# A two-layer encoder trunk in float32r: the first half of each down projection over 512 and 128 tokens instead of twice 320

## What is computed

```python
def _swiglu(x, w_gate, w_up, w_down):        # 1024 -> 2816 -> 1024
    return (jax.nn.silu(x @ w_gate) * (x @ w_up)) @ w_down
...
h = h + 0.5 * _rmsnorm(_swiglu(_rmsnorm(h, g[0]), f1g, f1u, f1d), g[1])
```

## Time and profile before

| what | value |
|---|---|
| median of 2 runs | 2795.7 us (2792.97 to 2798.44) |
| span of the profiled execution | 2795.9 us |
| PE busy | 2757.9 us, 99% |
| DVE busy | 1245.5 us, 45% |
| ACT busy | 849.1 us, 30% |
| POOL busy | 447.1 us, 16% |

### The profile page before, as it was taken

One profiled execution on the slowest core, in us unless ns is written; L12 is line 12 of the kernel. 1 busy time (PEld: TensorE's weight loads), 2 busy tenths in 40 slices (PEclk: granted clock), 3 DMA queues, 4 the chain that ended last, 5 costly groups with the idle time before them and its releaser, 6 DMA issues.

```text
span 2795.9 us, 54256 instructions
## 1 busy us (share of the span) xinstructions
PE 2757.9 (99%) x18682; PEld 2719.4 (97%) x18682; DVE 1245.5 (45%) x1997; ACT 849.1 (30%) x1331; POOL 447.1 (16%) x473
## 2 busy tenths in 40 slices
PE   8999999999999999999999999999999999999998
PEld 8999999989999999999999999999899999999997
DVE  5332333674444733233453333355644455333335
ACT  4221223333333522122332122233333343212223
POOL 3100112240001410011321001132300032100112
PEclk9999999999999999999999999999999999999998
DMA  3232222122223222222222222221122222222222
GB/s 104 75 90 86 73 82 71 48 61 66 74 73 91 59 73 81 66 75 87 65 70 75 83 83 75 86 73 50 46 75 75 77 76 61 75 83 76 74 79 89
DMA packets 425146, 208.44 MB, mean 75 GB/s; under 512 B 42425, under 2 KB 423323, under 8 KB 424987
## 3 DMA queue, kind: packets, MB, share of 16 engines
q1 hardware_dynamic: 421956, 203.46, 25.3%
q10 hardware_dynamic: 3062, 3.38, 0.4%
HBM read 203.28 MB, written 5.29 MB: 75 GB/s over the span
## 4 chain that ended last, share of the span: by engine, by line
PE 94%; DVE 3%; issue 1%; ACT 0%; POOL 0%; DVEq 0%; DMA 0%; SPq 0%; ACTq 0%; POOLq 0%
PE ps L540 30%; PE ps L541 29%; PE ps L542 29%; DVE h L1198 1%; DVE x_lo L1180 1%; PE ps L593 1%; PE ps L641 1%; PE ps L588 1%; PE ps L589 1%; PE ps L663 1%; PE ps L521 1%; DVE w_lo L1162 0%; PE ps L527 0%; POOL acc_y L1580 0%; PE ps L691 0%
## 5 line engine op out<-in xcount | busy, mean ns | idle before, releaser
L540 PE MATMUL ps<-x_hi,w_hi 128*128 128x320 f32 x3648 | 1136.6, 312 | 0.0
L542 PE MATMUL ps<-x_hi,w_lo 128*128 128x320 f32 x3648 | 1127.2, 309 | 0.0
L541 PE MATMUL ps<-x_lo,w_hi 128*128 128x320 f32 x3648 | 1127.0, 309 | 0.0
L540 PEld LDWEIGHTS ps<-x_hi,w_hi 128*128 128x128 f32 x3648 | 684.8, 188 | 11.4 <-issue 6.5
L541 PEld LDWEIGHTS ps<-x_lo,w_hi 128*128 128x128 f32 x3648 | 685.0, 188 | 0.2
L542 PEld LDWEIGHTS ps<-x_hi,w_lo 128*128 128x128 f32 x3648 | 684.8, 188 | 0.0
L858 ACT ACTIVATE w_hi<-raw 128x1024 fp32r<-128x1024 f32 (+1 forms) x326 | 362.3, 1114 | 758.8 <-PE ps L542 758.8
L1162 DVE TENSOR_TENSOR w_lo<-raw,w_hi 128x1024 fp32r<-128x1024 f32 (+1 forms) x326 | 423.4, 1300 | 179.9 <-ACT w_hi L858 179.9
L540 PE MATMUL ps<-mid_hi,w_hi 128*128 128x320 f32 x1232 | 382.0, 310 | 0.0
L541 PE MATMUL ps<-mid_lo,w_hi 128*128 128x320 f32 x1232 | 380.7, 309 | 0.0
L542 PE MATMUL ps<-mid_hi,w_lo 128*128 128x320 f32 x1232 | 380.7, 309 | 0.0
(11 more groups left out here) (199 smaller groups left out, 3001.1 us busy)
## 6 DMA issues: line engine op xcount, KB each, us to landing
raw<-in_ffn_w_gate_dram SPq DMA_DIRECT2D x360, 128.0 KB, 2.2
raw<-in_ffn_w_up_dram SPq DMA_DIRECT2D x360, 128.0 KB, 2.3
raw<-in_w_in_dram SPq DMA_DIRECT2D x304, 128.0 KB, 2.2
raw<-in_ffn_w_down_dram SPq DMA_DIRECT2D x192, 192.0 KB, 2.7
raw<-in_ffn_w_down_dram SPq DMA_DIRECT2D x64, 128.0 KB, 2.8
raw<-in_w_branch_dram SPq DMA_DIRECT2D x64, 128.0 KB, 2.6
raw<-in_w_out_dram SPq DMA_DIRECT2D x64, 128.0 KB, 2.3
rows<-in_x_prompt_dram SPq DMA_DIRECT2D x4, 512.0 KB, 5.3
```

The source lines that it names most:

```text
L540: pe.matmul(bank(b), wh, tile(xh, k, hf), start=k == ks[0], stop=False)
L541: pe.matmul(bank(b), wh, tile(xl, k, hf), start=False, stop=False)
L542: mm = pe.matmul(bank(b), wl, tile(xh, k, hf), start=False, stop=k == ks[-1])
```

## The change

In the first half (fg = 0) of each feed-forward block, a down group covers either the 512 prompt tokens (q = 0 and 1) or the 128 sample tokens (q = 2 and 3), where it was 320 and 320. The matmuls keep their number and their weights. The copies out of PSUM take the same widths. As the first group now reads columns of both old halves of mid, the wait for the last count of mid_split moves from the third group to the first; that at the third group is kept for fg = 1 only. The gate and up projections, the second half of the down projection and the mixer keep their two times 320 tokens.

```diff
+        def part(t, k, hf):
+            return t[:, k * NT:k * NT + SEQ] if hf == 0 else t[:, k * NT + SEQ:(k + 1) * NT]
...
                     wh, wl = (w_tile(i, where, s, k) for i in range(2))
+                    if wide:
+                        out, mh, ml = bank(b, (SEQ, NT - SEQ)[hf]), part(xh, k, hf), part(xl, k, hf)
+                    else:
+                        out, mh, ml = bank(b), tile(xh, k, hf), tile(xl, k, hf)
+                    pe.matmul(out, wh, mh, start=k == ks[0], stop=False)
+                    pe.matmul(out, wh, ml, start=False, stop=False)
+                    mm = pe.matmul(out, wl, mh, start=False, stop=k == ks[-1])
...
-                    pe.wait_ge(mid_split, unit + 2 * FG - 1)
+                    pe.wait_ge(mid_split, unit + 2 * FG - (1 if fg else 0))
                     pp, gg = down(0)
                     for q in range(4):
-                        if q == 2:
+                        if q == 2 and fg == 1:
                             pe.wait_ge(mid_split, unit + 2 * FG)
                             alone(pe)
-                        group(pp, gg + q, q % 2, q, (mid_hi, mid_lo), KF, q // 2)
+                        group(pp, gg + q, q % 2, q, (mid_hi, mid_lo), KF, q // 2, wide=fg == 0)
                     with pe.Fori(1, KD // 2 - 2 * fg) as i:
-                        pair_groups(*down(i), (mid_hi, mid_lo), KF)
+                        pair_groups(*down(i), (mid_hi, mid_lo), KF, fg == 0)
...
+            def take_part(i, q, g):
+                put_y(at_part(y_ffn, 2 * i + q % 2, q // 2), q, g, q, False, (SEQ, NT - SEQ)[q // 2])
```

More of the change, by code:

```diff
@@ L292, in tile, with at_part @@
             return t[:, k * NT:(k + 1) * NT] if hf is None else t[:, k * NT + hf * HT:k * NT + hf * HT + HT]
+        def part(t, k, hf):
+            return t[:, k * NT:k * NT + SEQ] if hf == 0 else t[:, k * NT + SEQ:(k + 1) * NT]
+        def at_part(t, k, hf):
+            return t[:, ds(k * NT + hf * SEQ, SEQ if hf == 0 else NT - SEQ)]
         def at_tile(t, k, hf):
@@ L527, in spread, with group @@
                 pe.matmul(bank(b), ones[0:SP_, :], diag[index % 2][0:SP_, :], start=True, stop=True).then_inc(spread_done, 1)
-            def group(pair, g, s, b, x, ks, hf, between=None, where="main"):
+            def group(pair, g, s, b, x, ks, hf, between=None, where="main", wide=False):
                 pe.wait_ge(w_split, 2 * pair + s + 3)
@@ L538, in group, with pair_groups @@
                         between(k)
[L539 to L542, removed]
+                    wh, wl = (w_tile(i, where, s, k) for i in range(2))
+                    if wide:
[5 more added lines that the diff above has]
+                    mm = pe.matmul(out, wl, mh, start=False, stop=k == ks[-1])
                 mm.then_inc(group_done, 1)
             K8, KF = range(KD), range(FG)
-            def pair_groups(pair, g, x, ks):
+            def pair_groups(pair, g, x, ks, wide=False):
                 for q in range(4):
-                    group(pair, g + q, q % 2, q, x, ks, q // 2)
+                    group(pair, g + q, q % 2, q, x, ks, q // 2, wide=wide)
             def first_four(pair, g, n, after_mixer):
@@ L1199, in new_h, with put_y @@
                                              in1=tile(h, k, hf), op0=ALU.mult, op1=ALU.add).then_inc(h_ready, 1)
-            def put_y(dst, q, g, n, add):
+            def put_y(dst, q, g, n, add, cols=HT):
                 dve.wait_ge(group_done, g + n + 1)
@@ L1207, in put_y @@
                 else:
-                    dve.tensor_copy(dst, bank(q)).then_inc(evac, 1)
+                    dve.tensor_copy(dst, bank(q, cols)).then_inc(evac, 1)
             def take_y(y, i, q, g, add):
                 put_y(at_tile(y, 2 * i + q % 2, q // 2), q, g, q, add)
+            def take_part(i, q, g):
+                put_y(at_part(y_ffn, 2 * i + q % 2, q // 2), q, g, q, False, (SEQ, NT - SEQ)[q // 2])
             def seam(n, y, add, pair, g, nk, where, pl, pn, gl, gn):
@@ L1324, in ffn @@
                         for q in range(4):
-                            take_y(y_ffn, i, q, gd + 4 * i, fg == 1)
+                            if fg == 0:
+                                take_part(i, q, gd + 4 * i)
+                            else:
+                                take_y(y_ffn, i, q, gd + 4 * i, True)
                             if q >= 2:
@@ L1329, in ffn @@
                         for q in range(4):
-                            take_y(y_ffn, KD // 2 - 1, q, gd + 2 * KD - 4, False)
+                            take_part(KD // 2 - 1, q, gd + 2 * KD - 4)
                             if q >= 2:
```

## The result

| kernel | median | ratio to before, 95% interval |
|---|---|---|
| before | 2795.7 us | |
| changed | 2872.2 us (2872.1 to 2872.3, 2 runs) | 1.0277 (1.0247 to 1.0306) |

The change costs 76.5 us; the forecast was 75. The page of the changed kernel: PE has 51 us more busy time, the other engines the same as in the earlier trace rows, and DVE, ACT and POOL stay far from the bound.

What follows compares the result with a forecast made beforehand. PE, busy for 99% of the span, was taken as the bound. Stream 47, wait 21.6 and clock 6.4 made 75 us on the profiled 2795.9: 2871 us, 2.7% slower, with a range of 2840 to 2950.

Steps and rivals of the forecast that it cites:

- Term 1, the stream: First-half down projections: a wide and a narrow matmul take 337.5 ns, 44.5 more than two equal ones; 47 us.
- the upper end, 234: Wide down matmul of 512 columns: 234.4 ns if all of the 146.5 scales with columns.
- the lower, 215: Wide down matmul of 512 columns: could cost 215 ns, going by plain float32 matmuls.
- Term 2, the wait: First down group waits for the end of the mid_lo chain, 5.4 us in each of four blocks; 21.6 us.
- Term 3, the clock: Behind each of the four waits, PE runs 3.41 us at half clock and loses 1.6 us; 6.4 us, from 0 to 13.
- Covered edits: Wider copies out of PSUM and slot 0's splitting behind the narrow group q = 3 stay hidden, 0.3 us to spare; nothing booked.
- fall in the narrow groups: Rival: half clock in the second half of each pair's 66 narrow matmuls; 83 us, 2954 us in all; chance 17%.
- stay at 146.5: Rival: narrow down matmuls still step at 146.5 ns, since their cost is mostly not columns; 2908 us; chance 8%.
- loads ran ahead: Rival: narrow matmuls follow at their columns' rate, 66.5 ns, so only the wait is paid; 2824 us; chance 9%.

Runs made afterwards that it cites:

- narrow_first: Changed kernel with 128 tokens in the first two groups and 512 in the other two, waits as before the change: 2842.1 us, ratio 1.0164.
- half_load_narrow: Changed kernel with only 64 of the 128 weight columns in the narrow groups: 2839.0 us, ratio 1.0156.
- load_96_narrow: Changed kernel with 96 of the 128 weight columns in the narrow groups: 2852.5 us (one run).
- load_32_narrow: Changed kernel with 32 of the 128 weight columns in the narrow groups: 2837.2 us (one run).
- wait_only: Kernel before, 320 and 320 tokens kept, with the wait for the last count of mid_split moved to the first down group: 2826.4 us, ratio 1.0106.
- mid_before_split: Changed kernel; in a first half's last gate and up pair DVE makes mid, and ACT mid_hi, ahead of splitting slot 1: 2859.2 us, ratio 1.0224.

## Why the prediction held, point by point

**Term 1, the stream** (47 us; 46.4 measured alone in narrow_first). The narrow step was taken as 0.111 us, nearest to four loads of attention scores; it is 111 ns, and half_load_narrow, load_96_narrow and load_32_narrow show that it is the load. The row of the scores did not show that: their operands q_t and k_t are plain float32 in the kernel, and plain float32 matmuls of 320 columns step at 0.269 us, so that those of 128 would take some 0.108 us by their stream alone (an estimate, in proportion to the columns). That its step was right all the same is luck; what bore the term is the float32r loads of lines 540 and 541, 0.11 us apart. That the cost starts where a load stops hiding, and not with the unevenness, is shown by 256 columns (no loss) beside 192 and 128 (the same 111 ns). The wide step was taken as 226.5 and is 228 ns; the upper end, 234, which scales all of the 146.5 ns with columns, is excluded, and so is the lower, 215.

The Trainium skill, page "TensorE: Matmul & The Clock Gate", section "LDWEIGHTS (loading the stationary operand)", gives a load as its columns / 1.2 in ns, 107 for 128 and 80 for 96; the runs here have steps of 111 and 85, so they agree with 4 to 5 ns on top. The Trainium skill's rule for a lone stream in the section "Back-to-back issue gap" of that page, which the prediction weighed and by which the split would be free, doesn't hold here: the split is free only down to 256 columns, and 256, 320 and 384 columns step at 120, 146.5 and 173 ns, 13 above their columns and not 2.5.

**Term 2, the wait** (21.6 us; 21.4 in the waits of the changed kernel and of wait_only). The chain that ends it is the predicted one, and mid_before_split shows its longest avoidable link.

**Term 3, the clock** (6.4 us; 7.6 by the 38 matmuls at half clock). wait_only puts terms 2 and 3 at 30.6 us together, 2.6 above the 28 predicted. The stretches at half clock were 3.2 to 5.3 us of work and not 3.41 each; the term was a little too small, within its bounds of 0 to 13. That it came so near is in part luck: it was sized by one seam of the kernel before, and another seam there, behind a wait of 2.66 us, stands at half clock three times as long, which would have put the term above its bound. A window of PE, kernel before:

```profile
499.89:510.13 10.24, 9.65 (x41) 0.50 0.46 104
```

That the clock makes up the difference between 30.6 and 21.4 is worked out from the steps at either level, 8.8 us in wait_only, and not tested by a run that holds the clock.

**Covered edits** (nothing booked; nothing seen). In the changed kernel the splitting of slot 0 ends just ahead of the next wide group, which starts at 210.46; rows of ACT and DVE:

```profile
206.98 1.38 ACT L868 ACTIVATE w_hi<-raw 128x1408 fp32r<-128x1408 f32 x1 [22.06 <-PE ps L552]
...
208.39 1.62 DVE L1172 TENSOR_TENSOR w_lo<-raw,w_hi 128x1408 fp32r<-128x1408 f32 x1 [1.00 <-ACT w_hi L868]
```

It ends at 210.01, with 0.45 us to spare where 0.3 was foreseen; half_load_narrow, whose narrow groups are shorter, shows the price once the cover is gone, 17.8 us at all 16 pairs.

**The rivals.** The clock does not fall in the narrow groups: their window is granted 1.00, though by the prediction's estimate the array streams columns for 53 of each 111 ns. The narrow step does not stay at 146.5. Nor does it fall below 93, as it would if loads ran ahead.

## What to carry to other kernels

In these runs a matmul hid the next weight load where its own step was the longer (256 columns, 120 ns, beside a load of 111); at 192 and 128 columns the step was the load, and narrowing from 192 to 128 gave nothing back. So split columns unevenly only as far as the smaller part still covers a load. Before widening a matmul, ask which producer its new columns come from: the wait moves to the start of the phase, with the chain of the last producer laid open. If it must move, put the work that the wait needs ahead of work that is needed later in the queues of that chain (3.1 of 5.4 us remained here), or begin with the part that is ready.

## What was not expected of the hardware

A float32r matmul of 256, 320 or 384 columns cost 13 ns above its columns at full clock (0.417 ns each), the same at 320 with 128 and with 64 weight columns loaded beside it. One of 128 columns, once its load is out of the way, cost 60 ns, which is only 7 above its 53. With 448 columns it was 16 (203 ns), with 512 it was 15 (228 ns). What sets this remainder is open. A stretch of 7.3 us with a narrow matmul every 111 ns kept full clock. Behind the waits of 5.4 us PE ran at half clock at all four places, in the changed kernel and in wait_only, and behind those of 3.1 us in mid_before_split at three of four.
